# MLP up projection with weight blocks stationary and tokens moving, on one Trainium2 core

## The chip, the cores and the metric

The kernel runs on one core of a Trainium2 chip. The metric is the device time of one execution, in microseconds (us). It was measured three times for the kernel before the change. One more execution was taken by the hardware profiler; all rows below come from that one.

## What is computed

Two transformer-like blocks follow one another on 256 tokens of width 2048, all in float32. Each block has a mixing part (projections, several mixers, gates, an output projection) and then an MLP. The change concerns only the two MLPs:

```python
# block 1
h = rms_norm(x, norm_mlp_g[l]) @ w_mlp_up[l]          # (256 x 2048) @ (2048 x 8192)
x = x + jnp.square(jax.nn.relu(h)) @ w_mlp_down[l]    # (256 x 8192) @ (8192 x 2048)
# block 2
h2 = rmsnorm(x, norm2_g[l])
x = x + jnp.square(jax.nn.relu(h2 @ w_mlp_in[l])) @ w_mlp_out[l]
return rmsnorm(x, final_g)
```

## The kernel before

**How a product is made.** Each float32 product is made of three products of the type fp32r (a shortened float32 that TensorE reads in one pass). Every operand is split into a high part and the rest: `whi` and `wlo` for the weights, `XH` and `XL` for the normed input, `YH` and `YL` (one tensor `Y`) for the hidden values. The sum is high x high, high x rest and rest x high.

**Units.** Weights stream from memory in units of 256 rows x 512 columns (512 KB), through a ring of `RING` = 4 buffers. For each unit SyncE issues the load into `raw` (`load`, L292), ScalarE copies it to `whi` (`hi`, L509 is the instruction's line), VectorE subtracts to get `wlo` (`lo`, L868), and TensorE multiplies (`unit`, matmuls on L1354). A buffer is loaded again when its `wlo` is made, and `whi` is overwritten when TensorE has finished the unit four back (the semaphore `units_multiplied`, called `used`).

**One unit on TensorE before.** `unit` holds a block of 128 tokens of the input stationary (it is loaded as TensorE's weights, 128 columns) and moves 512 columns of the weight matrix through. Per unit that is 2 halves of the contraction x 2 token blocks x 3 products = 12 matmuls of 512 columns, into the PSUM banks `PU` (banks 4 and 5), with tokens on partitions. Each matmul has a weight load (LDWEIGHTS) of its own.

**The MLP.** The 8192 hidden features are worked in `NF` = 16 chunks of 512. A chunk takes 8 units of up projection and 8 of down projection. The order on TensorE is: up of chunk 0; then a loop of 15 turns, where turn j does the up projection of chunk j+1 and then the down projection of chunk j; then the down projection of chunk 15. Down projection adds into `PA` (banks 0 to 3), and VectorE adds each result to `X` (`add`, L1270).

**Between up and down, before.** ScalarE takes relu of the two banks into `HB[0]` (`relu`, L509, two instructions of 128x512). VectorE squares into `HB[1]` (`square`, L1263). Both still have tokens on partitions, while the down projection needs features on partitions as its stationary operand. So TensorE transposes the chunk in 8 matmuls of 128x128 against `ident` (`split`, `pair`, L1357) into `PT` (banks 6 and 7), ScalarE copies the high part to `YH` (`split_pair`, L772) and VectorE subtracts the rest into `YL` (`split_lo`, L879), two instructions of 128x512 each. In the loop the 8 transposes stand in the middle of the up projection, after its fourth unit; for chunk 15 they stand alone, after the loop.

**What sets the order.** Every engine's program is written out by hand, in order. The waits are on semaphores between the engines; TensorE waits at the start of each turn for the relu of the chunk before (its banks are to be overwritten) and before each pair of down units for the addition that frees `PA`.

Of the kernel before, what the change touches and what calls it, by code (L numbers as in the profile page):

```python
# [15 lines left out]
F32 = mybir.dt.float32  # L16
# [33 lines left out]
def build(nc, A, out):  # L50
    with ExitStack() as ctx:
# [40 lines left out]
        PU = [banks[:, 4 + t, :] for t in range(NT)]  # L92
        PT = [banks[:, 6 + t, :] for t in range(NT)]

        off = [0]
# [30 lines left out]
        GB = slot(W, 8, 2)  # L126
        HB = [tok(slot(W, 4 + i)) for i in range(2)]
        M = tok(slot(W, 6, 4), D)
# [50 lines left out]
        for b in blocks:  # L179
            for ph in "ab":  # L180
                u0[b, ph] = u
                for ch in plan[b, ph]:
                    counts[ch.by] += 1
                    ch.n, ch.u0, ch.evicted = len(chunks), u, counts[ch.by]
                    chunks.append(ch)
                    find[(b,) + ch.tag] = ch
                    u += ch.nu
            u0[b, "m"] = u
            u += NF * 16
            down0[b] = counts["dve"]  # L190
            counts["dve"] += NF * NCH
            chunks += [None] * (len(chunks) % 2)
            ts0[b] = ts
            ts += 24 + 2 * NF
        evict = {"act": S("acc_read_by_act"), "dve": S("acc_read_by_dve")}
# [304 lines left out]
        def _(act):  # L500
# [267 lines left out]
            def mlp(b):  # L768
                H0 = ts0[b] + 24

                def split_pair(j, r):
                    act.wait_ge(ts_ready, j * 2 + (H0 + r + 1))  # L772
                    a(YH[:, UK * r:UK * r + UK, :], PT[r].rearrange("p (k t) -> p k t", t=T)).then_inc(S("ts_hi"), 1)

                def relu(base, n):

                    act.wait_ge(used, base + 8)
                    for t in range(NT):
                        ins = a(HB[0][:, t, :], PU[t], ACT.Relu)
                    ins.then_inc(S(f"relu{b}_ready"), 1)  # L780

                def body(j):
                    base = mlp_base(b, j)
                    for i in range(7):
                        hi(base, i)
                    split_pair(j, 0)
                    split_pair(j, 1)
                    for i in range(7, 12):
# [5 lines left out]
                hi_upto(u0[b, "m"] + 8)  # L794
                for i in range(4):
                    hi(mlp_base(b, 0), i)
                relu(u0[b, "m"], 0)
                base = mlp_base(b, 0)
                for i in range(4, 7):
                    hi(base, i)  # L800
                split_pair(0, 0)
                split_pair(0, 1)
                for i in range(7, 12):
                    hi(base, i)
                relu(base, 1)
                for i in range(12, 16):
                    hi(base, i)
                with act.Fori(1, NF - 1) as j:
                    body(j)
                base = mlp_base(b, NF - 1)  # L810
                for i in range(4):
                    hi(base, i)
                split_pair(NF - 1, 0)
                split_pair(NF - 1, 1)
# [41 lines left out]
        def _(dve):  # L856
# [401 lines left out]
            def mlp(b):  # L1258
                H0, base_evict = ts0[b] + 24, down0[b]

                def square(n):
                    dve.wait_ge(S(f"relu{b}_ready"), n + 1)
                    tt(HB[1], HB[0], HB[0], ALU.mult).then_inc(S(f"hidden{b}_ready"), 1)  # L1263

                def add(base, n):
# [5 lines left out]
                    ins.then_inc(evict["dve"], 1)  # L1271

                def split_pair(j, r):
                    split_lo(j * 2 + (H0 + r), r, YH[:, UK * r:UK * r + UK, :], YL[:, UK * r:UK * r + UK, :])

                def body(j, first):
# [9 lines left out]
                    else:  # L1286
                        add(last, 3)
                    for i in range(4, 7):
                        lo(base, i)
                    split_pair(j, 0)  # L1290
                    split_pair(j, 1)
                    for i in range(7, 12):
                        lo(base, i)
# [18 lines left out]
                add(last, 3)  # L1312
                split_pair(NF - 1, 0)
                split_pair(NF - 1, 1)
                lo(base, 4)
# [34 lines left out]
        def _(pe):  # L1350
# [288 lines left out]
            def mlp(b):  # L1639
                H0, e0 = ts0[b] + 24, down0[b]  # L1640
                H1, H2 = YH, YL

                def split(j, r):
                    pe.wait_ge(ts_split, j * 2 + (H0 + r - 1))
                    pair(None, r, HB[1], 2 * P * r)
# [9 lines left out]
                def body(j):  # L1655
                    base = mlp_base(b, j)
                    pe.wait_ge(S(f"relu{b}_ready"), j + 1)
                    for i in range(4):
                        unit(base, i, XH, XL, UK * i, PU, i == 0, False)
                    pe.wait_ge(S(f"hidden{b}_ready"), j + 1)  # L1660
                    split(j, 0)
                    split(j, 1)
                    for i in range(4, 8):
                        unit(base, i, XH, XL, UK * i, PU, False, i == 7)
                    down(j, base, 8)

                pairs = Steps(norm(ts0[b] + 16))
                for i in range(8):
                    pe.wait_ge(ts_split, ts0[b] + 16 + i + 1)
                    unit(0, u0[b, "m"] + i, XH, XL, UK * i, PU, i == 0, i == 7)  # L1670
                    pairs.upto(i)
                with pe.Fori(0, NF - 1) as j:
                    body(j)
                pe.wait_ge(S(f"hidden{b}_ready"), NF)
                split(NF - 1, 0)
                split(NF - 1, 1)
                down(NF - 1, mlp_base(b, NF - 1), 0)
# [52 lines left out]
```

## Time and profile before

| What | Value |
|---|---|
| Runs | 3228.06 us median of 3 (3226.01 to 3232.18) |
| Profiled execution, its span on the core (no other time of its own is given) | 3233.1 us |
| TensorE busy with matmuls | 3112.4 us, 96%, 13864 matmuls |
| TensorE weight loads | 2524.0 us, 78%, 13864 loads |
| VectorE / ScalarE / GpSimd busy | 1952.8 us (60%) / 1386.5 us (43%) / 458.1 us (14%) |
| Memory traffic | 589.39 MB, mean 182 GB/s |

The profiled execution's span lies 5.0 us above the median of the runs, or 0.16%. PE is TensorE with its matmuls, PEld its weight loads, DVE VectorE, ACT ScalarE, POOL GpSimd, SP SyncE. A matmul's recorded duration runs from its start to its modelled end, and matmuls overlap. So the time that one matmul costs in a stream is the distance between starts, not its duration. The times in a timeline are in us from the start of the span.

### The profile page before, as it was taken

To read this page: it belongs to the slowest core of one execution; us is meant where nothing else is said; L and a number is where in the kernel's file an instruction comes from. 1 tells how busy PE (TensorE), PEld (TensorE's weight loads), DVE (VectorE), ACT (ScalarE), POOL (GpSimd) and SP (SyncE) were. 2 spreads that over 40 slices of the span, in tenths; PEclk is the share of its full clock that TensorE was granted. 3 is DMA by queue.
4 is the path that set the end of the run, shared out by engine and by line. 5 is a ranking of instruction groups with operands and counts; after the bars stand their busy time and mean duration, and the time that the engine had idled before them with its cause. 6 is when DMAs were issued, how large, how long until landed. Compare 5 with 4: busy or idle time off the path is not lost.

```text
span 3233.1 us, 37776 instructions
## 1 busy us (share of the span) xinstructions
PE 3112.4 (96%) x13864; PEld 2524.0 (78%) x13864; DVE 1952.8 (60%) x2093; ACT 1386.5 (43%) x1613; POOL 458.1 (14%) x423
## 2 busy tenths in 40 slices
PE   6999999999899999999799999999998999999997
PEld 4777788888788888887676667888887888888886
DVE  3566655555777665665568775555555566656665
ACT  4444544444444444444343445444444444444443
POOL 2000101100688000000026550000000000000000
PEclk9999999999999999999899999999999999999999
DMA  5544666656566666665655445666655566666663
GB/s 159 163 139 139 198 206 192 194 175 215 183 214 208 218 188 189 189 188 177 180 163 158 143 133 163 206 215 200 201 195 165 181 190 188 188 188 190 192 188 130
DMA packets 300343, 589.39 MB, mean 182 GB/s; under 512 B 20840, under 2 KB 20944, under 8 KB 298832
## 3 DMA queue, kind: packets, MB, share of 16 engines
q1 hardware_dynamic: 291840, 562.11, 56.4%
q0 software_dynamic: 5760, 24.72, 2.4%
q10 hardware_dynamic: 2640, 1.18, 0.2%
q8 instruction: 66, 1.08, 0.1%
q14 instruction: 37, 0.30, 0.0%
HBM read 575.35 MB, written 12.58 MB: 182 GB/s over the span
## 4 chain that ended last, share of the span: by engine, by line
PE 87%; DVE 7%; ACT 2%; issue 2%; DMA 2%; ACTq 0%; POOL 0%; DVEq 0%; POOLq 0%
PE banks L1354 85%; DVE wlo L868 3%; PE banks L1357 2%; DMA raw<-in_w_in 1%; ACT whi L509 1%; DVE W L894 1%; ACT W L509 1%; DVE W L1270 0%; DMA x<-W 0%; ACTq L825 0%; DMA Z<-in_gm_w_s 0%; ACT L509 0%; DMA raw<-in_w_branch 0%; DVE W L1195 0%; DVE W L1200 0%
## 5 line engine op out<-in xcount | busy, mean ns | idle before, releaser
L868 DVE TENSOR_TENSOR wlo<-raw,whi 128x1024 fp32r<-128x1024 f32 x1048 | 1361.3, 1307 | 1028.8 <-ACT whi L509 1022.4
L509 ACT ACTIVATE whi<-raw 128x1024 fp32r<-128x1024 f32 x1048 | 1100.2, 1059 | 1258.4 <-PE banks L1354 1179.1
L1354 PE MATMUL banks<-whi,XH 128*128 128x512 f32 x2816 | 1125.8, 400 | 35.0 <-DVE wlo L868 30.5
L1354 PE MATMUL banks<-whi,XL 128*128 128x512 f32 x2816 | 1104.5, 392 | 0.0
L1354 PE MATMUL banks<-wlo,XH 128*128 128x512 f32 x2816 | 1104.4, 392 | 0.0
L1354 PE MATMUL banks<-whi,Y 128*128 128x512 f32 x2752 | 863.0, 391 | 10.8 <-DVE Y L879 8.0
L1354 PEld LDWEIGHTS banks<-whi,XH 128*128 128x128 f32 x2816 | 533.5, 189 | 173.7 <-DVE wlo L868 34.8
L1354 PEld LDWEIGHTS banks<-whi,XL 128*128 128x128 f32 x2816 | 532.8, 189 | 114.2
L1354 PEld LDWEIGHTS banks<-wlo,XH 128*128 128x128 f32 x2816 | 534.1, 190 | 105.7
L1354 PEld LDWEIGHTS banks<-whi,Y 128*128 128x128 f32 x2752 | 518.8, 189 | 120.5 <-DVE Y L879 8.4
L1354 PE MATMUL banks<-wlo,Y 128*128 128x512 f32 x1376 | 537.2, 390 | 0.0
L1354 PEld LDWEIGHTS banks<-wlo,Y 128*128 128x128 f32 x1376 | 259.6, 189 | 53.4
L1270 DVE TENSOR_TENSOR W<-banks,W 128x512 f32<-128x512 f32 x256 | 163.8, 681 | 7.9 <-PE banks L1354 7.9
L1357 PE MATMUL banks<-ident,W 128*128 128x128 f32 x616 | 91.2, 288 | 58.7 <-DVE W L894 40.0
L1357 PEld LDWEIGHTS banks<-ident,W 128*128 128x128 f32 x616 | 78.7, 149 | 73.8 <-issue 43.0
L484 POOL TENSOR_TENSOR W<-W 128x1024 f32<-128x1024 f32 x20 | 61.8, 3090 | 491.1 <-DVE W L929 491.1
L509 ACT ACTIVATE W<-banks 128x512 f32<-128x512 f32 (+1 forms) x138 | 74.3, 576 | 120.4 <-PE banks L1357 72.9
L509 ACT ACTIVATE Y<-banks 128x512 fp32r<-128x512 f32 (+1 forms) x80 | 41.7, 563 | 141.9 <-PE banks L1357 74.5
L495 POOL DMA_DIRECT2D x<-W x1 | 0.7, 705 | 501.8 <-DVE W L1270 501.8
L509 ACT ACTIVATE XH<-banks 128x512 fp32r<-128x512 f32 x48 | 27.5, 596 | 92.9 <-PE banks L1357 92.9
L879 DVE TENSOR_TENSOR Y<-banks,Y 128x512 fp32r<-128x512 f32 x64 | 41.2, 685 | 39.5 <-ACT Y L509 39.5
L879 DVE TENSOR_TENSOR XL<-banks,XH 128x512 fp32r<-128x512 f32 x48 | 31.8, 686 | 52.4 <-ACT XH L509 52.4
(234 smaller groups left out, 1224.4 us busy)
## 6 DMA issues: line engine op xcount, KB each, us to landing
raw<-in_w_in SPq DMA_DIRECT2D x384, 512.0 KB, 3.9
raw<-in_w_mlp_up SPq DMA_DIRECT2D x128, 512.0 KB, 3.8
raw<-in_w_mlp_down SPq DMA_DIRECT2D x128, 512.0 KB, 3.8
raw<-in_w_mlp_in SPq DMA_DIRECT2D x128, 512.0 KB, 3.8
raw<-in_w_mlp_out SPq DMA_DIRECT2D x128, 512.0 KB, 3.8
raw<-in_w_branch SPq DMA_DIRECT2D x80, 512.0 KB, 4.2
raw<-in_w_out SPq DMA_DIRECT2D x64, 512.0 KB, 4.5
tables<-G POOLq DMA_DIRECT2D x8, 1024.0 KB, 7.8
```

What stands on the lines that cost most here:

```text
L484: tt(m, m, TMP[added % 2], ALU.add).then_inc(S("tmp_added"), 1)
L495: pool.dma_start(A["x1"].rearrange("(t p) n -> p t n", p=P), X).then_inc(S("x_saved"), 16)
L509: return nc.scalar.activation(out_, in_, f, **kw)
L868: tt(wlo[:, i % RING, :], raw[:, i % RING, :], whi[:, i % RING, :].bitcast(F32), ALU.subtract)\
L879: tt(dst, PT[r].rearrange("p (k t) -> p k t", t=T), hi_.bitcast(F32), ALU.subtract).then_inc(ts_split, 1)
L894: ins = stt(XN[:, t, cols], X[:, t, cols], rs[:, t:t + 1], GB[:, cols], ALU.mult, ALU.mult)
L1270: ins = tt(x, PA[n % 2][t], x, ALU.add)
L1354: return nc.tensor.matmul(out_, l, r, start=start, stop=stop, **kw)
L1357: return nc.tensor.transpose(out_, in_, ident[:, :])
```

## The change

The up projection exchanges its operands. A block of 128 weight columns is now stationary, and all 256 tokens move through. The result has features on partitions, in the same two banks, now called `PH`: four pieces of 256 columns, one for each 128 features. It needs no transposes before the down projection. A unit is now 2 halves x 4 feature blocks x 3 products = 24 matmuls of 256 columns.

```diff
+        PH = banks[:, 4:6, :].rearrange("p b (f t) -> p (b f) t", t=T)
-        HB = [tok(slot(W, 4 + i)) for i in range(2)]
+        HF = [slot(W, 4 + i) for i in range(2)]
...
+            def unit_up(base, i, lh, ll, kt, first, last):
+
+                pe.wait_ge(lo_done, base + (i + 1))
+                for k in range(UK):
+                    for f in range(4):
+                        at = slice(CH * k + P * f, CH * k + P * f + P)
+                        w_hi, w_lo = whi[:, i % RING, at], wlo[:, i % RING, at]
+                        acc = PH[:, f, :]
+                        mm(acc, w_hi, lh[:, kt + k, :], start=first and k == 0 and f % 2 == 0, stop=False,
+                           skip_group_check=True)
+                        mm(acc, w_hi, ll[:, kt + k, :], start=False, stop=False, skip_group_check=True)
+                        ins = mm(acc, w_lo, lh[:, kt + k, :], start=False, stop=last and k == UK - 1,
+                                 skip_group_check=True)
+                ins.then_inc(used, 1)
```

On TensorE the loop loses its transposes and the wait for them:

```diff
                 def down(j, base, i0):
-                    pe.wait_ge(ts_split, j * 2 + (H0 + 2))
+                    pe.wait_ge(S(f"hidden{b}_split"), j + 1)
...
                     pe.wait_ge(S(f"relu{b}_ready"), j + 1)
-                    for i in range(4):
-                        unit(base, i, XH, XL, UK * i, PU, i == 0, False)
-                    pe.wait_ge(S(f"hidden{b}_ready"), j + 1)
-                    split(j, 0)
-                    split(j, 1)
-                    for i in range(4, 8):
-                        unit(base, i, XH, XL, UK * i, PU, False, i == 7)
+                    for i in range(8):
+                        unit_up(base, i, XH, XL, UK * i, i == 0, i == 7)
                     down(j, base, 8)
```

The high part of the hidden values is now a square that ScalarE takes of relu's result; VectorE squares as before and subtracts the high part in one instruction:

```diff
# ScalarE
-                def split_pair(j, r):
-                    act.wait_ge(ts_ready, j * 2 + (H0 + r + 1))
-                    a(YH[:, UK * r:UK * r + UK, :], PT[r].rearrange("p (k t) -> p k t", t=T)).then_inc(S("ts_hi"), 1)
...
-                    for t in range(NT):
-                        ins = a(HB[0][:, t, :], PU[t], ACT.Relu)
-                    ins.then_inc(S(f"relu{b}_ready"), 1)
+                    if not (isinstance(n, int) and n == 0):
+                        act.wait_ge(S(f"hidden{b}_squared"), n)
+                    a(HF[0], banks[:, 4:6, :].rearrange("p b c -> p (b c)"), ACT.Relu).then_inc(S(f"relu{b}_ready"), 1)
+                def square_hi(base, n):
+
+                    act.wait_ge(used, base)
+                    act.wait_ge(S(f"relu{b}_ready"), n + 1)
+                    a(hidden, HF[0], ACT.Square).then_inc(S(f"hidden{b}_hi"), 1)
# VectorE
                 def square(n):
                     dve.wait_ge(S(f"relu{b}_ready"), n + 1)
-                    tt(HB[1], HB[0], HB[0], ALU.mult).then_inc(S(f"hidden{b}_ready"), 1)
+                    if not (isinstance(n, int) and n == 0):
+                        dve.wait_ge(S(f"hidden{b}_split"), n)
+                    tt(HF[1], HF[0], HF[0], ALU.mult).then_inc(S(f"hidden{b}_squared"), 1)
+
+                def split(n):
+                    dve.wait_ge(S(f"hidden{b}_squared"), n + 1)
+                    dve.wait_ge(S(f"hidden{b}_hi"), n + 1)
+                    tt(rest, HF[1], hidden.bitcast(F32), ALU.subtract).then_inc(S(f"hidden{b}_split"), 1)
```

ScalarE takes `square_hi` at the head of a turn, before `hi` of unit 4, where its two copies stood after unit 6 before; its loop body now runs from unit 4 of one turn to unit 3 of the next. VectorE's `split` stands after `lo` of unit 4, where its two subtractions stood after unit 6. After the loop, `split` stands after the fourth addition, as the two subtractions did.

**TensorE, middle of the up projection in the loop of block 1.** Before (L1354 is a matmul of `unit`, with XH or XL stationary and `whi` or `wlo` moving; L1357 a transpose):

```order
L1354 MATMUL banks<-whi,XH 128x512
L1354 MATMUL banks<-wlo,XH 128x512
L1354 MATMUL banks<-whi,XL 128x512
L1644 ISA
L1357 MATMUL banks<-ident,W 128x128 x4
L1644 REGISTER_ALU
L1357 MATMUL banks<-ident,W 128x128 x4
L1361 REGISTER_ALU
L1354 MATMUL banks<-whi,XH 128x512
L1354 MATMUL banks<-wlo,XH 128x512
```

Now (L1341 is the matmul of `unit_up`), at a boundary between two units of the up projection:

```order
L1341 MATMUL banks<-XL,whi 128x256
L1341 MATMUL banks<-XH,wlo 128x256
L1358 REGISTER_ALU
L1341 MATMUL banks<-XH,whi 128x256
L1341 MATMUL banks<-XL,whi 128x256
L1341 MATMUL banks<-XH,wlo 128x256
```

The 8 transposes are gone, and each unit has 24 matmuls of half the width where it had 12.

**VectorE, after the loop of block 1.** Here the down projection of chunk 15 waits. Before (L868 makes `wlo`, L1270 adds to `X`, L879 makes `YL` from the transposes' banks):

```order
L868 TENSOR_TENSOR wlo<-raw,whi 128x1024 x2
L1270 TENSOR_TENSOR W<-banks,W 128x512 x2
L868 TENSOR_TENSOR wlo<-raw,whi 128x1024 x2
L1270 TENSOR_TENSOR W<-banks,W 128x512 x2
L879 TENSOR_TENSOR Y<-banks,Y 128x512 x2
```

Now (L854, L1263 and L1256 in their places):

```order
L854 TENSOR_TENSOR wlo<-raw,whi 128x1024 x2
L1263 TENSOR_TENSOR W<-banks,W 128x512 x2
L854 TENSOR_TENSOR wlo<-raw,whi 128x1024 x2
L1263 TENSOR_TENSOR W<-banks,W 128x512 x2
L1256 TENSOR_TENSOR Y<-W,Y 128x1024
```

The place is the same; two subtractions that read PSUM became one of twice the length that reads SBUF.

## Rows read from the trace of the kernel before

**Rows 1.** The profile page: busy time of each engine; granted TensorE clock in 40 slices.

```profile
PE 3112.4 (96%) x13864; PEld 2524.0 (78%) x13864; DVE 1952.8 (60%) x2093; ACT 1386.5 (43%) x1613; POOL 458.1 (14%) x423
...
PEclk9999999999999999999899999999999999999999
```

**Rows 2.** Windows: the loops of both MLPs; columns are us, busy us and instructions, PEclk.

```profile
1002.40:1491.10 488.70, 488.70 (x2201) 405.66 (x2201) 301.09 (x298) 208.17 (x221) 47.99 (x45) 1.00 0.63 194
2536.40:3158.40 622.00, 622.00 (x2801) 516.29 (x2801) 375.49 (x378) 264.94 (x281) 0.00 (x0) 1.00 0.62 189
```

**Rows 3.** Timeline of PE and PEld in the loop: two units' first matmuls, and loads.

```profile
1214.65 0.39 PE L1354 MATMUL banks<-whi,XH 128*128 128x512 f32 x1
1214.65 0.19 PEld L1354 LDWEIGHTS banks<-wlo,XH 128*128 128x128 f32 x1
...
1217.37 0.39 PE L1354 MATMUL banks<-whi,XH 128*128 128x512 f32 x1
```

**Rows 4.** Timeline of PE around the transposes of one loop turn, block 2.

```profile
2535.11 0.40 PE L1354 MATMUL banks<-whi,XL 128*128 128x512 f32 x1
2535.35 1.04 PE L1357 MATMUL banks<-ident,W 128*128 128x128 f32 x8
...
2536.45 0.39 PE L1354 MATMUL banks<-wlo,XH 128*128 128x512 f32 x1
```

**Rows 5.** Timeline of PE and PEld: fp32r matmuls of 256 columns, block 1.

```profile
59.32 0.28 PE L1354 MATMUL banks<-XH,wfh 128*8 128x256 f32 x1
...
61.89 0.28 PE L1354 MATMUL banks<-XH,wfl 128*8 128x256 f32 x1
...
64.73 0.28 PE L1354 MATMUL banks<-XL,wfh 128*8 128x256 f32 x1
64.73 0.19 PEld L1354 LDWEIGHTS banks<-whi,XH 128*128 128x128 f32 x1
64.84 0.40 PE L1354 MATMUL banks<-whi,XH 128*128 128x512 f32 x1
```

**Rows 6.** Timeline: four float32 matmuls of 128 columns with their loads, block 2.

```profile
1936.10 0.61 PE L1354 MATMUL banks<-SM,ident 128*128 128x128 f32 x4
...
1935.99 0.53 PEld L1354 LDWEIGHTS banks<-SM,ident 128*128 128x128 f32 x4
```

**Rows 7.** Timeline at the end of block 1's MLP loop, all engines.

```profile
1523.64 1.03 PE L1357 MATMUL banks<-ident,W 128*128 128x128 f32 x8
1523.90 1.06 ACT L509 ACTIVATE whi<-raw 128x1024 fp32r<-128x1024 f32 x1 [1.66 <-PE banks L1354]
...
1526.13 1.28 DVE L1270 TENSOR_TENSOR W<-banks,W 128x512 f32<-128x512 f32 x2
1527.33 1.28 DVE L879 TENSOR_TENSOR Y<-banks,Y 128x512 fp32r<-128x512 f32 x2
1528.66 0.50 PE L1354 MATMUL banks<-whi,Y 128*128 128x512 f32 x1 [3.99 <-DVE Y L879]
```

**Rows 8.** Groups by line: what TensorE, VectorE and ScalarE do per unit and chunk.

```profile
L868 DVE TENSOR_TENSOR wlo<-raw,whi 128x1024 fp32r<-128x1024 f32 x1048 | 1361.3, 1307 | 1028.8 <-ACT whi L509 1022.4
L509 ACT ACTIVATE whi<-raw 128x1024 fp32r<-128x1024 f32 x1048 | 1100.2, 1059 | 1258.4 <-PE banks L1354 1179.1
L1263 DVE TENSOR_TENSOR W<-W 128x1024 f32<-128x1024 f32 x32 | 44.9, 1403 | 0.0
```

**Rows 9.** Windows: after the stalls at the end of each MLP; PEclk is third from the end.

```profile
1528.60:1533.00 4.40, 4.34 (x12) 3.45 (x13) 0.01 (x1) 0.00 (x0) 0.00 (x0) 0.61 0.15 51
3195.90:3202.00 6.10, 6.05 (x15) 4.75 (x16) 0.00 (x0) 0.47 (x1) 0.00 (x0) 0.51 0.10 35
```

**Rows 10.** The profile page: the queue that fetches instructions; landing of an MLP load.

```profile
q8 instruction: 66, 1.08, 0.1%
...
raw<-in_w_mlp_up SPq DMA_DIRECT2D x128, 512.0 KB, 3.8
```

**Rows 11.** Waits of PE over the run: us in total, times, longest.

```profile
PE banks L1354 <- DVE W L1270: 2.1, 3, 1.0
```

More of the change, by code:

```diff
@@ L193, in build @@
             ts0[b] = ts
-            ts += 24 + 2 * NF
+            ts += 24
         evict = {"act": S("acc_read_by_act"), "dve": S("acc_read_by_dve")}
@@ L768, in mlp @@
             def mlp(b):
-                H0 = ts0[b] + 24
-                def split_pair(j, r):
-                    act.wait_ge(ts_ready, j * 2 + (H0 + r + 1))
-                    a(YH[:, UK * r:UK * r + UK, :], PT[r].rearrange("p (k t) -> p k t", t=T)).then_inc(S("ts_hi"), 1)
+                hidden = YH[:, 0:4, :].rearrange("p k t -> p (k t)")
                 def relu(base, n):
                     act.wait_ge(used, base + 8)
-                    for t in range(NT):
-                        ins = a(HB[0][:, t, :], PU[t], ACT.Relu)
-                    ins.then_inc(S(f"relu{b}_ready"), 1)
-                def body(j):
-                    base = mlp_base(b, j)
[L784 to L788, printed above, removed]
+                    if not (isinstance(n, int) and n == 0):
[5 more added lines that the diff above has]
+                    a(hidden, HF[0], ACT.Square).then_inc(S(f"hidden{b}_hi"), 1)
+                hi_upto(u0[b, "m"] + 8)
+                for i in range(4):
+                    hi(mlp_base(b, 0), i)
+                relu(u0[b, "m"], 0)
+                with act.Fori(0, NF - 1) as j:
+                    base = mlp_base(b, j)
+                    square_hi(base, j)
+                    for i in range(4, 12):
                         hi(base, i)
@@ L792, in body @@
                         hi(base, i)
-                hi_upto(u0[b, "m"] + 8)
-                for i in range(4):
[L796 to L809, printed above, removed]
+                    for i in range(16, 20):
+                        hi(base, i)
                 base = mlp_base(b, NF - 1)
[L811 to L814, printed above, removed]
+                square_hi(base, NF - 1)
                 for i in range(4, 8):
@@ L1258, in mlp @@
             def mlp(b):
-                H0, base_evict = ts0[b] + 24, down0[b]
+                hidden, rest = (m[:, 0:4, :].rearrange("p k t -> p (k t)") for m in (YH, YL))
                 def square(n):
                     dve.wait_ge(S(f"relu{b}_ready"), n + 1)
-                    tt(HB[1], HB[0], HB[0], ALU.mult).then_inc(S(f"hidden{b}_ready"), 1)
+                    if not (isinstance(n, int) and n == 0):
[5 more added lines that the diff above has]
+                    tt(rest, HF[1], hidden.bitcast(F32), ALU.subtract).then_inc(S(f"hidden{b}_split"), 1)
                 def add(base, n):
@@ L1271, in add @@
                     ins.then_inc(evict["dve"], 1)
-                def split_pair(j, r):
-                    split_lo(j * 2 + (H0 + r), r, YH[:, UK * r:UK * r + UK, :], YL[:, UK * r:UK * r + UK, :])
                 def body(j, first):
@@ L1287, in body @@
                         add(last, 3)
[L1288 to L1292, printed above, removed]
+                    lo(base, 4)
+                    split(j)
+                    for i in range(5, 12):
                         lo(base, i)
@@ L1312, in mlp @@
                 add(last, 3)
-                split_pair(NF - 1, 0)
-                split_pair(NF - 1, 1)
+                split(NF - 1)
                 lo(base, 4)
@@ L1639, in mlp @@
             def mlp(b):
-                H0, e0 = ts0[b] + 24, down0[b]
+                e0 = down0[b]
                 H1, H2 = YH, YL
-                def split(j, r):
-                    pe.wait_ge(ts_split, j * 2 + (H0 + r - 1))
-                    pair(None, r, HB[1], 2 * P * r)
                 def down(j, base, i0):
-                    pe.wait_ge(ts_split, j * 2 + (H0 + 2))
+                    pe.wait_ge(S(f"hidden{b}_split"), j + 1)
                     for i in range(8):
@@ L1657, in body @@
                     pe.wait_ge(S(f"relu{b}_ready"), j + 1)
-                    for i in range(4):
-                        unit(base, i, XH, XL, UK * i, PU, i == 0, False)
-                    pe.wait_ge(S(f"hidden{b}_ready"), j + 1)
-                    split(j, 0)
-                    split(j, 1)
-                    for i in range(4, 8):
-                        unit(base, i, XH, XL, UK * i, PU, False, i == 7)
+                    for i in range(8):
+                        unit_up(base, i, XH, XL, UK * i, i == 0, i == 7)
                     down(j, base, 8)
@@ L1669, in mlp @@
                     pe.wait_ge(ts_split, ts0[b] + 16 + i + 1)
-                    unit(0, u0[b, "m"] + i, XH, XL, UK * i, PU, i == 0, i == 7)
+                    unit_up(0, u0[b, "m"] + i, XH, XL, UK * i, i == 0, i == 7)
                     pairs.upto(i)
@@ L1673, in mlp @@
                     body(j)
-                pe.wait_ge(S(f"hidden{b}_ready"), NF)
-                split(NF - 1, 0)
-                split(NF - 1, 1)
                 down(NF - 1, mlp_base(b, NF - 1), 0)
```

## The prediction, on record before the changed kernel ran

> **What bounds the kernel now.** The page comes first: TensorE is busy for 96% of the span at the full clock almost everywhere, VectorE for 60%, ScalarE for 43% [rows 1]. That is an average, so the two MLP loops are read by themselves in windows. In both, PE is busy in every microsecond, at a granted clock of 1.00 (the 2.4 GHz level), with VectorE busy in 375.49 of 622.00 us and ScalarE in 264.94 [rows 2]. The MLP loops are bound by TensorE alone. What the change takes from TensorE there is gained in full, and what it adds is paid in full.
>
> The length of a turn follows from the windows: 622.00 us hold 14 turns (2801 matmuls = 14 x 200 + 1), and 488.70 us hold 11; both give 44.43 us [rows 2]. The timeline gives the price of a unit: from the first matmul of one to the first of the next is 1217.37 - 1214.65 = 2.72 us for 12 matmuls, so a matmul of 512 columns costs 226.7 ns [rows 3]. Sixteen units are 43.52 us. The 0.91 us left over is the 8 transposes: the timeline shows them between 2535.35 and 2536.14, with a slower first matmul after them [rows 4].
>
> **Removed: the transposes.** Each of the 15 turns of the two loops loses 0.91 us of TensorE: 30 x 0.91 = **-27.3 us**. The last chunk of each MLP has its transposes too, but they stand in a chain there [rows 7]. They run at 1523.64, ScalarE copies, VectorE makes two additions (1526.13) and then the two subtractions (1527.33), and TensorE goes on at 1528.66. The additions wait for the end of the down projection before them, and not for the transposes. After the change the same additions stand there, then one subtraction of 1024 columns. Its nearest rows are the square of the same length, 1.40 us in the mean over all turns [rows 8], and the pair it replaces, 1.28 us [rows 7]. ScalarE's square is ready sooner: it follows the copy of 1523.90, and two instructions of 1.06 us end near 1526.0. So TensorE goes on at about the same time, and the transposes here are worth 0. I take 0, with 0.1 us to either side.
>
> **Added: twice as many matmuls, of half the width.** The up projections are 16 chunks x 8 units x 2 blocks = 256 units, or 6144 matmuls of 256 columns in place of 3072 of 512. If cost went purely by columns, each would cost half of 226.7, 113.3 ns, and the term would be 0. A price per instruction would be paid twice as often. Every nanosecond above 113.3 costs 6144 x 0.001 = 6.1 us, and this is the number that decides the case.
>
> The trace has one stream of the same kind: 48 matmuls of fp32r with 256 columns moving, in block 1 [rows 5]. From 59.32 to 64.73 they are 47 steps: 115.1 ns each. The first 22 steps (to 61.89) took 116.8 ns, the last 25 took 113.6. They differ from the new ones in the weight load: 8 columns, where the new ones load 128. The last of them had a 128-column load behind it: that load started at 64.73, with the matmul, and the next matmul started at 64.84, 0.11 us later. So the load fits under a 256-column matmul, once at least. Four matmuls with 128-column loads and about 107 ns of streaming each ran (0.61 - 0.28) / 3 = 0.11 us apart, their loads likewise (0.53 - 0.19) / 3 [rows 6]. So loads can follow each other every 0.11 us, for four in a row.
>
> I take 115.1 ns, the mean of the nearest stream. A unit then costs 24 x 0.1151 = 2.762 us, 0.042 more, times 256 units = **+10.9 us**. The lower bound is 113.3 ns (0 us); nothing in the rows speaks for less. The upper bound is 120 ns: that is half of the streaming time, 106.7, plus the whole excess of a 512-column matmul over its columns at 2.4 GHz, 226.7 - 213.3 = 13.4. It costs 24 x 0.120 = 2.88, 0.16 more per unit, +41.0 us.
>
> The Trainium skill, "TensorE: Matmul & The Clock Gate", section "Back-to-back issue gap", gives N / 2.4 plus about 2.5 ns for a stream at full clock. The row for 512 columns is 226.7 ns where that rule gives 215.8, so the trace does not agree on the size. Taken for the fixed part alone, the rule makes the term 3072 x 2.5 ns = 7.7 us in place of 10.9.
>
> **Moved work on the other engines.** ScalarE: two copies of 128x512 leave, a square of 128x1024 comes, about as long as a `whi` copy, 1.06 us; the relu becomes one instruction of the same 1024 columns. VectorE: a pair of 1.28 us leaves, an instruction of 1.2 to 1.4 us comes [rows 7, 8]. Both engines keep their idle time in the loop [rows 2], so this costs 0. The new waits also cost nothing inside the loop. `square_hi` waits for the end of the down projection before it, as the `whi` copy before it does; behind it stand the copies for unit 4 on. If it and the split come 5 us late, as the chain at the end takes, the down projection that needs them is still 8 units, 22 us, away. Should that cover fail, the cost would be at most those 5 us in a turn. The loads of SyncE's queue keep their order and number.
>
> **Two small places.** In the first turn of block 1 GpSimd still works, and TensorE waited 2.1 us in all for additions there and elsewhere [rows 11]; a longer SBUF subtraction could double that: 0 to +2.1 us, taken as 0. After the stall that ends each MLP the granted clock was 0.61 of full over 4.40 us and 0.51 over 6.10 us [rows 9]: near the lower level of 1.2 GHz. Those 12 and 15 matmuls would have taken 2.7 and 3.4 us at 226.7 ns, so the low clock cost 1.7 + 2.7 = 4.4 us. The stall keeps its length, but the clock may come back earlier or later: -4.4 to +4.4, taken as 0.
>
> **Sum.** -27.3 + 10.9 = -16.4 us. The profiled execution's 3233.1 us becomes 3216.7. Its span is 5.0 us above the median of the runs, so against the median the forecast is 3228.06 - 16.4 = **3211.7 us**, 0.5% faster. About 0.2%, 6.5 us, is what a measurement of this kernel can tell from no change. A gain above that needs the matmul under 116.7 ns; a loss above it needs over 118.8.
>
> **Rivals.**
> 1. The stream runs at its slower pace: 116.8 ns, as the first 22 steps did [rows 5]. For it: while TensorE's queue is being filled, matmuls seem a little slower (after the transposes too [rows 4]), and twice the instructions fill it all the time. Against it: the later 25 steps ran at 113.6. The term is (2.803 - 2.72) x 256 = 21.3 us, the sum -6.0, the time 3222: no change that can be told.
> 2. Slower: the excess goes with the instruction and the 128-column load, 120 ns. For it: the only long streams with 128-column loads are those of 512 columns, and the load has now hardly more than its own time to hide in. Against it: the single step of 0.11 us at 64.73. The time is 3228.06 - 27.3 + 41.0 = 3241.8. It decides from 118.8 ns on.
> 3. The weight load does not overlap at all. The timeline speaks plainly against it: the next load starts at 1214.65 with the matmul, and the stream keeps 226.7 ns, only 13.4 over the streaming [rows 3]. Were 0.11 us of load [rows 6] added to each of the 6144 matmuls, it would be +676 us, less 27.3: 3877 us. The Trainium skill, "TensorE: Matmul & The Clock Gate", section "Part 3: Packing small matmuls — row/col tiling", says that loads overlap running matmuls only where the row groups differ, which would forbid it here. The trace disagrees.
> 4. The loop body outgrows the store of instructions. It grows from 200 to 288 matmuls, each with its load. Instructions came in 66 packets in the whole run [rows 10], too few for 15 passes of each loop, so the old body stays loaded. If the new one did not, each of the 28 jumps back would wait for something like a landing, 3.8 us [rows 10]: +106 - 16.4, 3318 us. The Trainium skill, "Runtime: NRT & Kernel Launch", section "Instruction fetch mechanics", says that a jump outside two pages of 16 KiB stalls, and also that TensorE's store holds 2048 instructions. By the second the new body fits.
> 5. By columns alone, 113.3 ns: -27.3, 3200.8 us.
>
> **How the numbers follow.** The matmul below 116.7 ns, with my forecast and rival 5 in it: 0.66. Between 116.7 and 118.8, rival 1: 0.16. Above: rival 2 0.14, rival 3 0.01, rival 4 0.03, together 0.18. The range goes from rival 5 less 2 us for the clock, 3199, to 3238, which is 119.4 ns. Below it I leave 0.05, above it 0.13.
>
> **What would show it.** The 256-column matmuls of the MLPs start 115 ns apart, their loads too, and a unit takes 2.76 us. A loop turn takes 8 x 2.762 + 8 x 2.72 = 43.86 us in place of 44.43. There are 16680 matmuls (13864 - 256 + 3072). PE stays busy in the whole loop and waits for no one. At the end of each MLP it still stands still for about 5 us, now from the last matmul on. I am wrong if the step is off by over 2 ns, or if PE shows idle time at the head of a turn or before a down projection.

## The result, and the profile after

The changed kernel takes 3243.99 us (median of 5 runs, 3242.82 to 3244.63), the kernel before 3228.06 us (5 runs, 3225.88 to 3232.18). The medians differ by 15.9 us. The ratio of the runs is 1.0043, with a 95% interval of 1.0030 to 1.0055, which is slower by 13.9 us, between 9.7 and 17.8. The forecast of 3211.7 us had the wrong sign, and the time lies above its range. It lies 2 us from rival 2, 3241.8.

Lines of the profile page: the span, the busy time of each engine, the clock row, the queue of instructions and one of the three groups of new matmuls:

```profile
span 3241.5 us, 43302 instructions
PE 3122.9 (96%) x16680; PEld 2657.4 (82%) x16680; DVE 1951.7 (60%) x2061; ACT 1383.9 (43%) x1549; POOL 461.9 (14%) x423
PEclk9999999999999999999899999999999999999999
q8 instruction: 68, 1.11, 0.1%
L1341 PE MATMUL banks<-XH,whi 128*128 128x256 f32 x2048 | 581.9, 284 | 4.4 <-ACT W L510 4.4
```

TensorE is as full as before [rows 1], at the full clock, with 16680 matmuls. Instructions came in 68 packets, 2 more than before [rows 10]. The two loops, as windows (columns: window, length, busy time and count of PE, PEld, DVE, ACT, POOL, then the granted clock, the DMA share and GB/s):

```profile
1069.40:1528.70 459.30, 459.30 (x2928) 419.44 (x2928) 274.86 (x269) 192.15 (x184) 0.00 (x0) 1.00 0.60 189
2527.70:3200.20 672.50, 672.50 (x4320) 615.72 (x4320) 398.92 (x389) 281.32 (x269) 0.00 (x0) 1.00 0.59 187
```

They answer to [rows 2]. In block 2, 4320 matmuls are 15 turns of 192 + 96; 672.50 / 15 = 44.83 us a turn, where 44.43 stood before and 43.86 was forecast. TensorE has no idle time in either window, so within them nothing waits. The matmuls themselves take the time. The timeline of TensorE, the first two up matmuls of a turn, the last one, and the first down matmul:

```profile
2662.23 0.28 PE L1341 MATMUL banks<-XH,whi 128*128 128x256 f32 x1
2662.34 0.28 PE L1341 MATMUL banks<-XL,whi 128*128 128x256 f32 x1
...
2685.14 0.28 PE L1341 MATMUL banks<-XH,wlo 128*128 128x256 f32 x1
2685.26 0.40 PE L1341 MATMUL banks<-whi,Y 128*128 128x512 f32 x1
```

Between 2662.23 and 2685.26 lie 192 matmuls: 23.03 / 192 = 0.1199 us. The step is **120.0 ns**, not 115.1. The very first step, behind a 512-column matmul, is shorter, 0.11 us (2662.23 to 2662.34), and is not the pace of the stream. The loads keep pace, each starting with a matmul; this is the timeline of PEld:

```profile
1099.83 0.19 PEld L1341 LDWEIGHTS banks<-XL,whi 128*128 128x128 f32 x1
1099.95 0.19 PEld L1341 LDWEIGHTS banks<-XH,wlo 128*128 128x128 f32 x1
1100.07 0.19 PEld L1341 LDWEIGHTS banks<-XH,whi 128*128 128x128 f32 x1
```

The end of the first MLP, as the chain of waits:

```profile
1527.85 0.92 PE banks L1341 x4
1528.77 0.02 issue
1528.79 1.06 ACT whi L510
1529.86 0.02 issue
1529.88 0.97 DVE wlo L854
1530.85 0.17 issue
1531.02 1.28 DVE W L1263 x2
1532.30 1.14 DVE Y L1256
1533.44 0.04 issue
1533.49 1.61 PE banks L1341 x3
```

Two additions and then one subtraction of 1.14 us, in place of the pair of [rows 7]. From the last matmul's start, 1528.37 on the timeline, to the next one's, 1533.49, are 5.1 us.

### The profile page after: what moved, and what is told of

It reads as the page before. It is cut to its first block, busy times and chain, and to the rows that moved or that the text cites. A ratio compares the mean times of both kernels' runs of the same rounds, so it can differ in the third digit from the quotient of the medians.

```text
span 3241.5 us, 43302 instructions
## 1 busy us (share of the span) xinstructions
PE 3122.9 (96%) x16680; PEld 2657.4 (82%) x16680; DVE 1951.7 (60%) x2061; ACT 1383.9 (43%) x1549; POOL 461.9 (14%) x423
## 4 chain that ended last, share of the span: by engine, by line
PE 88%; DVE 6%; issue 2%; ACT 2%; DMA 1%; ACTq 0%; POOL 0%; DVEq 0%; SPq 0%; POOLq 0%
PE banks L1341 87%; DVE wlo L854 2%; PE banks L1344 1%; ACT whi L510 1%; DVE W L880 1%; ACT W L510 1%; DMA raw<-in_w_in 0%; DVE W L1263 0%; DMA x<-W 0%; DMA raw<-in_w_mlp_down 0%; ACTq L811 0%; ACT L510 0%; DMA Z<-in_gm_w_s 0%; DVE W L1181 0%; DVE W L1186 0%
## 5 line engine op out<-in xcount | busy, mean ns | idle before, releaser
L854 DVE TENSOR_TENSOR wlo<-raw,whi 128x1024 fp32r<-128x1024 f32 x1048 | 1360.8, 1306 | 1078.6 <-ACT whi L510 1075.6
L1341 PE MATMUL banks<-whi,Y 128*128 128x512 f32 x2752 | 863.1, 391 | 12.3 <-DVE Y L1256 9.5
L1341 PE MATMUL banks<-whi,XH 128*128 128x512 f32 x1792 | 720.9, 402 | 27.0 <-DVE wlo L854 27.0
L1341 PE MATMUL banks<-wlo,XH 128*128 128x512 f32 x1792 | 704.2, 393 | 0.0
L1341 PE MATMUL banks<-whi,XL 128*128 128x512 f32 x1792 | 703.8, 393 | 0.0
L1341 PEld LDWEIGHTS banks<-whi,Y 128*128 128x128 f32 x2752 | 518.5, 188 | 122.4 <-DVE Y L1256 10.3
L1341 PE MATMUL banks<-XH,whi 128*128 128x256 f32 x2048 | 581.9, 284 | 4.4 <-ACT W L510 4.4
L1341 PE MATMUL banks<-XL,whi 128*128 128x256 f32 x2048 | 581.1, 284 | 0.0
L1341 PE MATMUL banks<-XH,wlo 128*128 128x256 f32 x2048 | 581.0, 284 | 0.0
L1341 PE MATMUL banks<-wlo,Y 128*128 128x512 f32 x1376 | 537.3, 390 | 0.0
L1341 PEld LDWEIGHTS banks<-whi,XH 128*128 128x128 f32 x1792 | 340.0, 190 | 125.0 <-DVE wlo L854 29.3
L1341 PEld LDWEIGHTS banks<-whi,XL 128*128 128x128 f32 x1792 | 339.5, 189 | 73.9
L1341 PEld LDWEIGHTS banks<-XH,whi 128*128 128x128 f32 x2048 | 394.8, 193 | 5.9 <-issue 4.8
L1341 PEld LDWEIGHTS banks<-XL,whi 128*128 128x128 f32 x2048 | 394.8, 193 | 1.1
L1341 PEld LDWEIGHTS banks<-wlo,XH 128*128 128x128 f32 x1792 | 340.2, 190 | 66.7
L1341 PEld LDWEIGHTS banks<-XH,wlo 128*128 128x128 f32 x2048 | 394.7, 193 | 0.0
L1341 PEld LDWEIGHTS banks<-wlo,Y 128*128 128x128 f32 x1376 | 259.5, 189 | 52.2
L1263 DVE TENSOR_TENSOR W<-banks,W 128x512 f32<-128x512 f32 x256 | 163.8, 681 | 7.9 <-PE banks L1341 7.9
L1344 PE MATMUL banks<-ident,W 128*128 128x128 f32 x360 | 58.1, 299 | 58.8 <-DVE W L880 40.1
```

The costliest lines, as they stand in the source:

```text
L854: tt(wlo[:, i % RING, :], raw[:, i % RING, :], whi[:, i % RING, :].bitcast(F32), ALU.subtract)\
L1263: ins = tt(x, PA[n % 2][t], x, ALU.add)
L1341: return nc.tensor.matmul(out_, l, r, start=start, stop=stop, **kw)
L1344: return nc.tensor.transpose(out_, in_, ident[:, :])
```

## The experiments

All of them ask what a matmul of an up projection costs, or what its surroundings cost. Where no number of rounds is given, a variant ran once, and its whole time is known only to within the spread of single runs (6.3 us over five runs of the kernel before); those readings rest on steps in the trace. A step is read as above: first up matmul to first down matmul, divided by the number of up matmuls. Where unit 0 of a chunk keeps its full shape, its 24 matmuls (2.88 us) are taken off, and 168 are left. Four theories of the 120.0 ns stood against each other. *Instruction*: every matmul pays about 13 ns. *Load*: a 128-column load pays it. *Width*: the price goes in some other way with the 256 columns. *Exchange*: it lies in what is stationary and what moves.

### 64 columns loaded

```diff
+                        C = P if first else 64
-                        at = slice(CH * k + P * f, CH * k + P * f + P)
-                        acc = PH[:, f, :]
+                        at = slice(CH * k + P * f, CH * k + P * f + C)
+                        acc = PH[0:C, f, :]
```

> The changed kernel with only 64 weight columns stationary in each up matmul (units 1 to 7 of a chunk; unit 0 keeps 128), 256 tokens moving as before; half of each chunk's features get only the first unit's share, so the output is not the block's. The step between 256-column matmuls tells the theories apart. Load theory (the 128-column weight load sets the pace): 113 to 116 ns in units 1 to 7, 120 in unit 0. Instruction theory (about 13.3 ns for each matmul over its columns, whatever it loads): 120 ns everywhere, the time unchanged at 3244 us. Sum theory (a fixed part plus a part that grows with loaded columns, through 115.1 ns at 8 columns and 120 at 128): 117.4 ns.

Measured: 3209.74 us, the kernel before beside it 3229.07.

```profile
2642.16 0.28 PE L1341 MATMUL banks<-XH,whi 128*128 128x256 f32 x1
...
2664.08 0.40 PE L1341 MATMUL banks<-whi,Y 128*128 128x512 f32 x1
```

(21.92 - 2.88) / 168 = 113.3 ns. The excess is halved by a smaller load with the number of instructions unchanged. The price does not hang on the instruction alone. The edit does a second thing: the result covers 64 partitions of PSUM in place of 128. No run parts this from the shorter load, here and wherever fewer columns are loaded.

### 8 columns loaded

The same edit with `C = P if first else 8`, the shape of the 48 matmuls that the forecast was taken from [rows 5].

> As the run with 64 columns, but 8 stationary columns in units 1 to 7: the very shape of the 48 matmuls of block 1 that the prediction took its price from, now in a long stream. Load theory: 113 to 116 ns. Instruction theory: 120 ns. Sum theory: 115.1 ns. If it is 116.8 for good, the faster half of the old stream was the exception.

Measured: 3228.51 us beside 3229.07.

```profile
2654.94 0.28 PE L1341 MATMUL banks<-XH,whi 128*128 128x256 f32 x1
...
2677.41 0.40 PE L1341 MATMUL banks<-whi,Y 128*128 128x512 f32 x1
```

(22.47 - 2.88) / 168 = 116.6 ns. So the shape I had priced at 115.1 costs 116.6 in a long stream: the first 22 steps of [rows 5] were its price, the last 25 an exception. And a load of 8 columns costs more than one of 64, so the price does not simply grow with the length of the load either.

### 128 columns moving

```diff
+                        N = T if first else P
-                        acc = PH[:, f, :]
+                        acc = PH[:, f, 0:N]
```

and `0:N` columns of `lh` and `ll` in the three matmuls.

> The changed kernel with 128 weight columns stationary and only 128 of the 256 tokens moving in units 1 to 7 of a chunk (the rest of the tokens get only unit 0's share). Load theory: the step stays at 112 to 120 ns though the streaming is halved to 53 ns. Instruction or sum theory: 53.3 + 13.3 = 67 ns, unless the load then takes over at about 112. A step of 120 as with 256 columns would make the load the whole price; 107 to 113 would say that load and streaming each fit alone and disturb each other when both fill the time.

Measured: 3205.33 us beside 3229.07.

```profile
2640.58 0.28 PE L1341 MATMUL banks<-XH,whi 128*128 128x256 f32 x1
...
2643.46 0.22 PE L1341 MATMUL banks<-XH,whi 128*128 128x128 f32 x1
2643.52 0.28 PE L1341 MATMUL banks<-XL,whi 128*128 128x128 f32 x1
...
2662.05 0.28 PE L1341 MATMUL banks<-XH,wlo 128*128 128x128 f32 x1
2662.17 0.44 PE L1341 MATMUL banks<-whi,Y 128*128 128x512 f32 x1
```

(21.59 - 2.88) / 168 = 111.4 ns, and a whole unit of narrow matmuls takes 2.68 us on the timeline, 111.7 for each. Half the columns save only 8 ns. It is not the narrow matmul that needs this long: the first one was followed after 0.06 us (2643.46 to 2643.52), and only then came the steps of 0.11. So I read about 112 ns as the pace at which loads of 128 columns followed each other. The 0.11 us of [rows 6] could not show it, since about 107 ns of streaming stood beside those loads. But 112 is below 120, so the load's own pace doesn't set the price of the 256-column matmul.

### The kernel before with matmuls of 256 columns

Tokens stay stationary and the transposes stay; only each 512-column matmul is cut in two.

```diff
+                        for h in range(2):
+                            cols = slice(T * h, T * h + T)
...
+                                ins = mm(acc[t][:, cols], l[:, kt + k, P * t:P * t + P],
+                                         w[:, i % RING, CH * k + T * h:CH * k + T * h + T],
```

> The kernel before with its up matmuls cut in two halves of 256 columns: tokens stationary, weights moving, transposes kept, result unchanged. All theories: 120 ns per matmul, since width and load are those of the change; time before + 41 us, about 3269. If instead the step is near 113.3 and the time near 3228, the price is in exchanging the operands (weights as stationary side), not in the width.

Measured: 3269.68 us beside 3229.07: +40.6.

```profile
1200.00 0.28 PE L1354 MATMUL banks<-whi,XL 128*128 128x256 f32 x1
...
1201.20 0.28 PE L1354 MATMUL banks<-whi,XH 128*128 128x256 f32 x1
...
2633.12 0.28 PE L1354 MATMUL banks<-whi,XH 128*128 128x256 f32 x1
...
2678.80 0.28 PE L1354 MATMUL banks<-whi,XH 128*128 128x256 f32 x1
```

Ten steps in 1.20 us, 120 ns, and a turn of 2678.80 - 2633.12 = 45.68 us where 44.43 stood: 30 turns x 1.25, and 1.28 for the first chunk of each MLP, make 40.1 us. This is the added term alone; rival 2 had it at 41.0. The exchange of operands costs nothing in the step. It is the cutting in two that costs.

### The other half alone: no transposes, old up projection

```diff
-                        unit_up(base, i, XH, XL, UK * i, i == 0, i == 7)
+                        unit(base, i, XH, XL, UK * i, PU, i == 0, i == 7)
...
```

The same edit stands before the loop, for chunk 0.

> The changed kernel with the up matmuls of the kernel before (tokens stationary, 512 columns moving) and still no transposes, so the transposition of the hidden values is left out of the computation. It measures the removed part alone. My term: 30 loop turns x 0.91 us = 27.3 us less than before, 3200.8 us, a turn of 43.52 us, and the stall at the end of each MLP as long as with the change. Rival: the transposes were partly hidden, so less than 20 us is gained.

Measured in 5 rounds: 3208.12 us (3205.94 to 3209.19) beside 3231.28 (3226.17 to 3234.66); the ratio is 0.9927, interval 0.9913 to 0.9940, so -23.6 us, between -28.1 and -19.4. The timeline has a turn of block 2 at 43.52 us from down to down, as 16 x 2.72 gives. But block 1 has two turns that GpSimd works in, of 48.09 and 45.09 us: 6.1 us over, where before had 45.38 and 46.45, 3.0 over its 44.43. Those 3.1 us are most of the 3.7 missing from 27.3; the interval holds 27.3 as well, so the trace and not the runs shows the loss. What stretches such turns shows in the groups of VectorE, first from 875 to 1099 us (block 1), then from 2600 to 2824 (block 2), then in two parts of the first stretch:

```profile
L854 DVE TENSOR_TENSOR wlo<-raw,whi 128x1024 fp32r<-128x1024 f32 x81 | 127.6, 1588 | 56.8 <-ACT whi L510 56.6
L1263 DVE TENSOR_TENSOR W<-banks,W 128x512 f32<-128x512 f32 x40 | 25.5, 678 | 0.0
```

```profile
L854 DVE TENSOR_TENSOR wlo<-raw,whi 128x1024 fp32r<-128x1024 f32 x83 | 101.8, 1226 | 86.4 <-ACT whi L510 86.4
L1263 DVE TENSOR_TENSOR W<-banks,W 128x512 f32<-128x512 f32 x42 | 26.9, 682 | 0.0
```

The two parts, 876 to 931 us and 1056.5 to 1099 us, with their windows (PE, PEld, DVE, ACT, POOL, clock, DMA share, GB/s):

```profile
L854 DVE TENSOR_TENSOR wlo<-raw,whi 128x1024 fp32r<-128x1024 f32 x20 | 32.4, 1632 | 13.3 <-ACT whi L510 13.3
876.00:931.00 55.00, 53.27 (x236) 43.77 (x234) 43.27 (x32) 25.91 (x25) 52.19 (x52) 1.00 0.65 206
```

```profile
L854 DVE TENSOR_TENSOR wlo<-raw,whi 128x1024 fp32r<-128x1024 f32 x16 | 19.6, 1223 | 15.5 <-ACT whi L510 15.4
1056.50:1099.00 42.50, 41.51 (x182) 33.73 (x181) 26.19 (x26) 17.01 (x17) 0.00 (x0) 1.00 0.77 254
```

From 875 to 1099 us, where GpSimd is busy for most of the time, the subtractions that read only SBUF took 1588 ns in the mean instead of 1226; the additions, which read PSUM, did not change (678 and 682). Memory traffic is not the reason: where GpSimd stood idle the subtractions took 1223 ns at 254 GB/s, and where it was busy 1632 ns at 206 GB/s. An addition behind them was late, and TensorE waited, on the timeline:

```profile
931.94 0.49 PE L1341 MATMUL banks<-whi,Y 128*128 128x512 f32 x1 [2.67 <-DVE W L1263]
```

After it the granted clock was 0.83 over the window from 931 to 941 us. With less work on TensorE per turn, VectorE has less time to be done in. That this is why more is lost here than before is my reading; no run took GpSimd away. The changed kernel, with its turns of 46.01, 46.57 and 45.88 us, lost 4.0 us there.

### The two products of `whi` in one instruction

`whi` is loaded once and `XH` and `XL` move behind it as 512 columns, into two halves of a bank; then one matmul of 256 for `wlo`. ScalarE and VectorE add the halves.

```diff
+                        mm(banks[:, 4 + f, :].rearrange("p (h t) -> p h t", t=T), whi[:, i % RING, at], XX[:, :, kt + k, :],
+                           start=first and k == 0, stop=False, skip_group_check=True)
+                        ins = mm(banks[:, 4 + f, 0:T], wlo[:, i % RING, at], XH[:, kt + k, :], start=False,
```

> A version meant to beat both: with w_hi stationary, XH and XL move in one matmul of 512 columns into one PSUM bank per 128 features (two regions of 256), w_lo x XH is a matmul of 256 columns into the first region; ScalarE copies the second region out and VectorE adds it, relu follows. Chunk 0 of each MLP is as in the change. Per loop unit 8 x (226.7 + 120) = 2.773 us against 2.88 in the change and 2.72 before: a turn of 8 x (2.773 + 2.72) = 43.95 us. Against the change 30 x 0.88 = 26 us less, 3218 us, 0.3% faster than before. If the excess of a matmul depends on its load alone and the 256-column matmul between two wide ones gets its load hidden (113.3 ns), 3205. If PE starts to wait for the longer chain (copy, add, relu, square), it is above 3228.

Measured in 5 rounds: 3238.11 us (3232.49 to 3241.48), ratio 1.0017 (1.0008 to 1.0026). By their ratios to the kernel before, it beats the changed kernel (1.0043) but not the one before, and the 3218 expected for it did not come.

```profile
2660.55 0.39 PE L1360 MATMUL banks<-XX,whi 128*128 128x512 f32 x1
2660.78 0.28 PE L1360 MATMUL banks<-XX,wlo 128*128 128x256 f32 x1
2660.89 0.40 PE L1360 MATMUL banks<-XX,whi 128*128 128x512 f32 x1
...
2683.15 0.40 PE L1360 MATMUL banks<-whi,Y 128*128 128x512 f32 x1
```

22.60 / 64 = 353 ns a pair, where 226.7 + 120.0 = 346.7 would be the sum of the two shapes. A turn took 44.39 us, 0.44 more than expected and only 0.04 less than before, and the turns beside GpSimd, 45.91, 46.71, 48.64 and 45.87, took that back and more.

### The same pair, with `XH` and `XL` side by side

```diff
-        XX = sb("XX", [P, 2, KD, T], F32R)
+        XX = sb("XX", [P, KD, 2 * T], F32R)
```

> As the paired version, but XH and XL of a feature block lie side by side, so the 512 columns that move past w_hi are one run of memory, and the output is one whole bank. The paired version measured 236 ns for the wide matmul of two runs of 256 and 117 for the narrow one behind it, 353 per pair. If the two runs were the reason: 226.7 + 113 to 120, 340 to 347 ns per pair, a turn 0.05 to 0.1 us x 8 shorter, 30 x 0.4 to 0.8 = 12 to 25 us less than the paired version, 3213 to 3226: at last below the kernel before. If the step depends on the widths alone, 353 ns again and 3238 us. Either way the input is now read in two runs when XH or XL is split or used as the stationary side; 128 contiguous columns each, so no change there.

Measured in 5 rounds: 3238.85 us (3234.07 to 3239.26) beside 3232.35, ratio 1.0016 (1.0007 to 1.0025); a turn again 44.39 us. Where the halves of the input lie in memory makes no difference that shows. What makes the pair 6 ns dearer than its parts stays open.

### 512 columns moving, 64 loaded

`no_transposes` with `C = P if first else 64` columns of the input stationary.

> The kernel without transposes, its up matmuls with 64 of 128 tokens stationary and 512 columns moving in units 1 to 7 (half of the tokens get only unit 0's share). Load theory: nothing changes, 226.7 ns, since the load was hidden under 512 columns. Sum theory: 226.7 less 64 x 0.041 = 224 ns. Instruction theory: 226.7.

Measured: 3214.93 us; no_transposes on the same chip had 3208.12.

```profile
2646.90 0.39 PE L1341 MATMUL banks<-whi,XH 128*128 128x512 f32 x1
...
2668.94 0.39 PE L1341 MATMUL banks<-whi,Y 128*128 128x512 f32 x1
```

(22.04 - 2.72) / 84 = 230.0 ns, against 226.7 with 128 columns loaded. The smaller load that saved 6.7 ns at 256 columns costs 3.3 here. No single price for a load of a given length fits both.

### 384 columns moving

The kernel before, with `N = CH if first else 384` columns moving.

> The kernel before with 384 of 512 weight columns moving in units 1 to 7 of a chunk's up projection (the last 128 features of a chunk get only unit 0's share); loads of 128 columns, transposes kept. So far 512 columns cost 226.7 ns and 256 columns 120.0, both 13.3 over their columns at 2.4 GHz. Fixed theory (13.3 ns on every matmul with a 128-column load): 160 + 13.3 = 173.3 ns. Width theory (6.25% over the columns where the load is well covered, and something more of its own at 256 columns, where load and streaming are nearly equal): 170 ns.

Measured: 3111.82 us beside 3232.35.

```profile
1199.80 0.33 PE L1354 MATMUL banks<-whi,XH 128*128 128x384 f32 x1
...
1201.53 0.33 PE L1354 MATMUL banks<-wlo,XH 128*128 128x384 f32 x1
```

Ten steps in 1.73 us: 173 ns. From 256 to 512 columns the step grows by 226.7 - 120.0 = 106.7 ns, 0.417 ns a column, which is one column for each period of 2.4 GHz. By this 384 columns stream in 160.0 ns, and 13 are over. With 120.0 - 106.7 and 226.7 - 213.3 there are three widths, and all three leave about 13.3 ns.

### 96 columns loaded

`C = P if first else 96` in the first edit.

> The changed kernel with 96 weight columns stationary in units 1 to 7 (a quarter of each chunk's features get only unit 0's share). Steps so far: 116.7 ns at 8 columns, 113.3 at 64, 120.0 at 128. If the price comes from a load that is nearly as long as the streaming, 96 columns (a load shorter by some 27 ns) should be at 113.3. If every loaded column beyond 64 costs its share, 116.7. If 120, only narrow loads are cheap.

Measured: 3226.09 us beside 3232.35.

```profile
2652.84 0.28 PE L1341 MATMUL banks<-XH,whi 128*128 128x256 f32 x1
...
2675.20 0.40 PE L1341 MATMUL banks<-whi,Y 128*128 128x512 f32 x1
```

(22.36 - 2.88) / 168 = 116.0 ns. With 8, 64, 96 and 128 columns loaded the step is 116.6, 113.3, 116.0 and 120.0. From 64 on that is near an even share for each further column, for which 116.7 was expected; 8 columns do not fit it.

### The same operands every time

```diff
-                        at = slice(CH * k + P * f, CH * k + P * f + P)
+                        at = slice(CH * k + P * f, CH * k + P * f + P) if first else slice(0, P)
```

and `kt + k if first else 0` for the moving tokens.

> The changed kernel in which all up matmuls of units 1 to 7 load the first 128 columns of their unit's buffer and move the same 256 columns of XH or XL (the input's first 128 features), so the output is not the block's. Width, load and number are those of the change. If the 120 ns come from which addresses the load and the streaming read, the step changes (113.3 or more than 120). If they come from the sizes alone, it stays at 120.0 and the time at 3244 us.

Measured: 3243.00 us, as the changed kernel.

```profile
2661.91 0.28 PE L1341 MATMUL banks<-XH,whi 128*128 128x256 f32 x1
...
2684.94 0.40 PE L1341 MATMUL banks<-whi,Y 128*128 128x512 f32 x1
```

23.03 / 192 = 120 ns. The addresses that are read don't matter.

## Why the prediction was wrong

**The step that failed** is "I take 115.1 ns, the mean of the nearest stream", the term of +10.9 us. It measured 120.0 ns and +41.0 us: 256 units x 0.16. With it the sum is 3228.06 - 27.3 + 41.0 = 3241.8, or 13.7 us slower. The ratio says 13.9 us; against the median of 3243.99 us 2.2 are left, which the interval of the ratio covers.

What misled was the choice of the row. I had two: a stream of the right width with a load of 8 columns [rows 5], and the long streams with the right load and twice the width [rows 3]. I took width for the thing that matters. The 384-column run shows that with 128-column loads the excess does not depend on width, so [rows 3] gave the price: 106.7 + 13.4. The prediction had this very sum, and used it only as its upper bound. The stream of [rows 5] misled twice. Its load is another one, and its second half, at 113.6 ns, did not last in a longer stream: there the same shape ran at 116.6. Even a perfect reading of it would have given 3222, rival 1. The evidence that I set against rival 2 was a single step of 0.11 us behind a 128-column load. One step, read to 0.01 us, can hardly tell 113 from 120, and a first step is no sign of the stream: the changed kernel, too, begins with 0.11 us and goes on at 0.12.

**Removed: -27.3 us** is right in the loop: without transposes and with the old matmuls a turn takes 43.52 us. In the whole kernel 23.6 arrived (19.4 to 28.1), and the trace has 3.1 us that went back in the turns beside GpSimd. I had taken those as 0 with a bound of +2.1. The changed kernel lost 4.0 us there by its turn lengths, 1.0 more than the kernel before. So this term was mis-sized too, but within its bound.

**Moved work: 0** held. TensorE has no idle time in the two windows. The end of the first MLP is 5.1 us from the last matmul's start to the next one's, where before 5.25 lay between the last one ahead of the transposes (1523.41 on the timeline) and 1528.66 on [rows 7], and the subtraction took 1.14 us, below the 1.2 to 1.4 of the forecast. `XH,whi` at the head of the first turn waited 4.4 us in total for relu, in both MLPs together. The prediction had idle time there as a sign of being wrong, but the kernel before has the same wait, on its list of the waits of TensorE:

```profile
PE banks L1354 <- ACT W L509: 4.5, 2, 2.3
```

So it is not a cost of the change.

**The clock after the stalls: 0** held within 1 us. Over the first 4.40 us after the stall of block 1 (1533.40 to 1537.80) the granted clock was 0.61, as before [rows 9], and from that restart to the next transposes 29.17 us passed in both kernels (1533.49 to 1562.66, and 1528.66 to 1557.83). In block 2 the last matmul started 23.8 us after the restart, where 24.4 stood before.

**The other rivals.** Rival 1, 116.8 ns, is about what an 8-column load costs (116.6), and 3222 is far off. Rival 3 would have given 3877 us. Rival 4 fell by 68 packets: the longer body of the loop, 288 matmuls and 288 loads, stays loaded. The Trainium skill, "Runtime: NRT & Kernel Launch", section "Instruction fetch mechanics", gives two sizes for TensorE's store, 2048 instructions and two pages of 16 KiB; this trace agrees with the larger. Rival 5, columns alone, fell by every stream with 128-column loads. As for the rule of the Trainium skill, "TensorE: Matmul & The Clock Gate", section "Back-to-back issue gap" (N / 2.4 plus about 2.5 ns): its form is right for 128-column loads at the three widths, its constant is not. The prediction called it a rule for a stream. The section itself gives it for a matmul by itself and has about 131 ns for a stream of loads and matmuls at N = 512, and this trace, at 226.7 ns, does not agree with that either. With the measured 13.3 in the place of 2.5 the added term is 3072 x 13.3 = 41 us.

**Open** is the mechanism of the 13.3 ns. It is neither the instruction alone (64 columns loaded: 113.3), nor the pace of the loads (about 112), nor the addresses, nor which operand is stationary, nor a price by the load's length (64 columns are better at 256 moving and worse at 512). It depends on the load and the stream together, and perhaps on how many partitions of PSUM are written; these runs give its values, not its cause.

## What to carry to other kernels

Price a matmul from the longest stream with the same load, and, for 128-column loads, take the columns at the full clock and a fixed excess apart: cutting a bound stream into narrower matmuls pays that excess once more for each, here 13.3 ns x 3072 = 41 us for 27.3 us of transposes. When the forecast hangs on a few ns of a step, run the old kernel with only the shape changed; one such run, `tokens_stationary_256`, gave 40.6 us in its time and 40.1 by its turns for a term of 41. What is saved on the engine that bounds a stage can be lost again in turns where another engine is already nearly late: look at those turns by themselves.

## What was not expected of the hardware

- With 128-column loads a matmul of this type took 120.0, 173.3 and 226.7 ns at 256, 384 and 512 columns: the columns at 2.4 GHz and 13.3 ns each time.
- The step of a 256-column matmul does not rise evenly with the load: 116.6, 113.3, 116.0 and 120.0 ns at 8, 64, 96 and 128 columns. At 512 columns moving, 64 loaded took 230.0 ns and 128 took 226.7.
- At 128 columns moving, which stream in 53.3 ns at 2.4 GHz, the step was still 111.7 ns, though the first such matmul was followed after 0.06 us: there the load is the bound, by my reading.
- Beside a busy GpSimd, subtractions of VectorE that read SBUF took 1632 ns in the mean, and 1223 in the same block with GpSimd idle and more memory traffic. Its additions from PSUM took 678 ns over the stretch with GpSimd and 682 without.
